# Decoder layer kernel: merge, output and down projections in token-major form, up projection on joined high and low halves

## The chip, the cores and the metric

The kernel runs on one core of a Trainium2 chip. The metric is the device time of one execution in microseconds (us); less is better.

## What is computed

One layer with 256 tokens, 2048 channels, all in fp32. In the reference, cut to what matters here:

```python
h = modulate(rms_norm(x, norm1_gain), shift1, scale1)
aq, ak, av, gq, gk, gv, gr, glr, ga, gb = split(h @ w_in)        # 2048 x 11792
merged = sigmoid(ga) * (y_attn @ w_branch_attn) + sigmoid(gb) * (y_gla @ w_branch_gla)
x = x + gate1 * (merged @ w_out)                                  # 2048 x 2048
h2 = modulate(rms_norm(x, norm2_gain), shift2, scale2)
u = h2 @ w_ffn_up                                                 # 2048 x 11264
y = conv_b + sum(conv_w[tap] * shifted(u, tap) for tap in 0..2)   # causal over tokens
a, b = split(y); x = x + gate2 * ((silu(a) * b) @ w_ffn_down)     # 5632 x 2048
```

shift, scale and gate (six vectors of 2048) come from `silu(c) @ w_ada + b_ada`, a vector times a 2048 x 12288 matrix.

## The kernel before

Every large product is done in units. A unit is 256 rows (two k-tiles of 128) by 512 columns of a weight matrix, 512 KB. SP loads it to one of four slots of `stage`; ScalarE rounds it to fp32r (`w_hi`, helper `hi`, L525); VectorE (DVE) subtracts (`w_lo`, helper `lo`, L766); TensorE multiplies. Activations are split in the same way into a high and a low half, and each product is three matmuls: hi x hi, lo x hi, hi x lo. SP may load unit k when the low half of unit k-4 is made (`lo_done`), ScalarE may round it when TensorE has used unit k-4 (`used`). The four engines run programs of their own, in an order written out by hand, which meet at semaphores.

In the *feature* form the weights stand in the array (128 columns at a time) and 256 tokens stream: 24 matmuls of 256 columns a unit (`unit`, L1161). In the *token* form, used for the GLA values, the activations of 128 tokens stand and 512 weight columns stream: 12 matmuls of 512 columns. The result of the first is channels by tokens, of the second tokens by channels. Results lie in two halves of PSUM (`ps`, parity `par`), each freed by `ps_free`.

The order: norm and modulation; queries and keys; GLA queries, keys, values; attention between them; the GLA gate; then **merge** (4 turns of 28 units: gate a, gate b, attention branch, GLA branch; L1406), **output** (2 turns of 16 units, L1423), the second norm, **up** (11 turns of 16 units, L1442) and **down** (2 turns of 44 units, L1453). Beside the units the modulation is accumulated: tiles `ada` of w_ada (512 KB each, 192 in all) are multiplied by c on DVE (`times_c`, L777) and added up over partitions by TensorE (`reduce_mod`, L1195), 16 tiles to a chunk of 1024 values; chunks 7 to 10 go beside the merge, chunk 11 beside the output projection. After each merge turn ScalarE and DVE split the merged tiles (`m_hi`, L700, `m_lo`, L1034). `x` is stored in feature order to HBM early (L393) and re-read into `x1` for the residual, which SP issues 12 units ahead of the output projection (L440). After the output projection the squares are summed (ScalarE L711, DVE L1063 and L1066), TensorE adds them over partitions, ScalarE makes the root, and tile by tile DVE, ScalarE and DVE again make `h2_hi` and `h2_lo` (L1082, L721, L793), each freeing one unit of the up projection's first block. In the up projection ScalarE and DVE take the convolution straight from PSUM (L737, L1104, L1108). In the down projection DVE adds gate and residual (L1136), TensorE transposes the result to token order (`back`, L1456), ScalarE copies it (L537), SP stores it.

## Time and profile before

| | |
|---|---|
| time, median of 3 runs | 1770.29 us (1768.89 to 1773.26) |
| span of the profiled execution | 1765.9 us (the page gives no other time of it) |
| TensorE, matmuls, busy | 1652.6 us, 94% |
| DVE busy | 1137.1 us, 64% |
| ScalarE busy | 775.7 us, 44% |
| HBM read | 384.26 MB, 221 GB/s over the span |
| mean granted clock of TensorE | 0.961 of full speed |

Matmuls are pipelined, and their ends are modelled: a record of 0.28 us may follow the last one after 0.12. So the price of one is the length of an unbroken stretch over its number. The granted clock is 1.00 or 0.50 of full speed (2.4 or 1.2 GHz). "Issue" is time in which an engine waited for nothing that the profile shows.

### The profile page before, as it was taken

Reading aid. Unit: us, or ns where it says so; the run is one execution under the profiler, and the core shown is the slowest. Engines: PE = TensorE matmul, PEld = TensorE weight load, DVE = VectorE, ACT = ScalarE, POOL = GpSimd, SP = SyncE. Lnnn points to the kernel's source line nnn. Section 1 sums busy time; section 2 is a strip of 40 time slices with the busy share of each in tenths; the row PEclk is TensorE's granted clock in tenths of the full one; section 3 lists DMA queues with packets and bytes.
Section 4 is the critical chain, followed back from the end, with each engine's and each line's share of the span. In section 5 each row is a group of like instructions: output and inputs, shape, how many; then the busy total and the mean of one; then the engine's idle time right before and its main releaser. Section 6 shows DMA issues by size and latency. Waiting matters only on the chain.

```text
span 1765.9 us, 33321 instructions
## 1 busy us (share of the span) xinstructions
PE 1652.6 (94%) x13089; PEld 1617.8 (92%) x13089; DVE 1137.1 (64%) x1192; ACT 775.7 (44%) x906; POOL 78.9 (4%) x52
## 2 busy tenths in 40 slices
PE   3185999999999999999999899999999999999999
PEld 3185999877999999999999899999999999998998
DVE  5797366598787686767687666666666555544443
ACT  3022433576675434333344545444445444433332
POOL 3052000000121000000000000000000000000000
PEclk8596899999999999999999899999999999999999
DMA  8978658576667878878888466666666666656553
GB/s 262 344 255 284 229 191 274 184 245 208 210 216 233 285 277 286 289 274 295 277 303 276 134 186 179 182 185 179 182 186 179 182 186 180 183 170 196 173 165 129
DMA packets 180117, 390.79 MB, mean 221 GB/s; under 512 B 13970, under 2 KB 18622, under 8 KB 179534
## 3 DMA queue, kind: packets, MB, share of 16 engines
q1 hardware_dynamic: 180046, 389.82, 68.7%
q8 instruction: 48, 0.79, 0.2%
q14 instruction: 23, 0.19, 0.0%
HBM read 384.26 MB, written 5.25 MB: 221 GB/s over the span
## 4 chain that ended last, share of the span: by engine, by line
PE 88%; DVE 6%; DMA 4%; ACT 1%; issue 1%; SPq 0%; DVEq 0%; ACTq 0%
PE ps L1144 83%; PE b L1144 5%; DMA ada<-in_w_ada 3%; DVE acc L777 3%; DVE acc_odd L777 1%; DVE h_lo L793 1%; DMA vrows<-in_ffn_conv_w 0%; DVE xn L818 0%; DMA stage<-in_w_in 0%; DVE w_lo L766 0%; PE b L1315 0%; PE ps L1223 0%; ACT w_hi L525 0%; PE b L1460 0%; ACT p L644 0%
## 5 line engine op out<-in xcount | busy, mean ns | idle before, releaser
L766 DVE TENSOR_TENSOR w_lo<-stage,w_hi 128x1024 fp32r<-128x1024 f32 x512 | 628.7, 1231 | 509.3 <-ACT w_hi L525 507.0
L525 ACT ACTIVATE w_hi<-stage 128x1024 fp32r<-128x1024 f32 x528 | 556.4, 1058 | 798.7 <-PE ps L1144 685.8
L1144 PE MATMUL ps<-h_hi,w_hi 128*128 128x256 f32 x2528 | 722.7, 286 | 16.6 <-DVE h_lo L793 16.6
L1144 PE MATMUL ps<-h_lo,w_hi 128*128 128x256 f32 x2528 | 718.9, 284 | 0.0
L1144 PE MATMUL ps<-h_hi,w_lo 128*128 128x256 f32 x2528 | 718.7, 284 | 0.0
L1144 PEld LDWEIGHTS ps<-h_hi,w_hi 128*128 128x128 f32 x2528 | 488.5, 193 | 18.8 <-issue 12.0
L1144 PEld LDWEIGHTS ps<-h_lo,w_hi 128*128 128x128 f32 x2528 | 488.6, 193 | 0.9 <-issue 0.8
L1144 PEld LDWEIGHTS ps<-h_hi,w_lo 128*128 128x128 f32 x2528 | 488.5, 193 | 0.0
L777 DVE SCALAR_TENSOR_TENSOR acc<-ada,cact,acc 128x1024 f32<-128x1024 f32 x156 | 220.8, 1415 | 6.5 <-DMA ada<-in_w_ada 3.8
L1144 PE MATMUL ps<-g_hi,w_hi 128*128 128x256 f32 x704 | 200.6, 285 | 4.1 <-issue 4.1
L1144 PE MATMUL ps<-g_lo,w_hi 128*128 128x256 f32 x704 | 200.2, 284 | 0.0
L1144 PE MATMUL ps<-g_hi,w_lo 128*128 128x256 f32 x704 | 200.2, 284 | 0.0
L1144 PEld LDWEIGHTS ps<-g_hi,w_hi 128*128 128x128 f32 x704 | 136.2, 193 | 4.3 <-issue 4.3
L1144 PEld LDWEIGHTS ps<-g_lo,w_hi 128*128 128x128 f32 x704 | 136.2, 193 | 0.0
L1144 PEld LDWEIGHTS ps<-g_hi,w_lo 128*128 128x128 f32 x704 | 136.1, 193 | 0.0
L1144 PE MATMUL ps<-m_hi,w_hi 128*128 128x256 f32 x256 | 72.6, 284 | 0.0
L1144 PE MATMUL ps<-m_lo,w_hi 128*128 128x256 f32 x256 | 72.5, 283 | 0.0
L1144 PE MATMUL ps<-m_hi,w_lo 128*128 128x256 f32 x256 | 72.5, 283 | 0.0
L1144 PE MATMUL ps<-yg_hi,w_lo 128*128 128x256 f32 x256 | 72.5, 283 | 0.0
L1144 PE MATMUL ps<-yg_lo,w_hi 128*128 128x256 f32 x256 | 72.5, 283 | 0.0
L1144 PE MATMUL ps<-yg_hi,w_hi 128*128 128x256 f32 x256 | 72.5, 283 | 0.0
L1144 PE MATMUL ps<-w_hi,h_hi 128*128 128x512 f32 (+1 forms) x160 | 62.1, 388 | 0.0
(231 smaller groups left out, 1699.6 us busy)
## 6 DMA issues: line engine op xcount, KB each, us to landing
ada<-in_w_ada SPq DMA_DIRECT2D x192, 512.0 KB, 5.1
stage<-in_w_in SPq DMA_DIRECT2D x184, 512.0 KB, 4.1
stage<-in_w_ffn_up SPq DMA_DIRECT2D x176, 512.0 KB, 3.7
stage<-in_w_ffn_down SPq DMA_DIRECT2D x88, 512.0 KB, 4.5
...
x_tok<-in_x SPq DMA_DIRECT2D x1, 2048.0 KB, 7.6
```

The costliest lines, as they stand in the source:

```text
L525: act.activation(w_hi[:, u.slot(k)], stage[:, u.slot(k)], ACT.Copy).then_inc(hi_done, 1)
L766: TT(w_lo[:, u.slot(k)], stage[:, u.slot(k)], w_hi[:, u.slot(k)].bitcast(F32), ALU.subtract).then_inc(lo_done, 1)
L777: STT(out=to[:], in0=ada[:, a.slot(k)], scalar=cc, in1=to[:], op0=ALU.mult, op1=ALU.add).then_inc(ada_done, 1)
L793: f = STT(out=x_lo[:, kt], in0=xn(kt), scalar=shift(kt), in1=x_hi[:, kt].bitcast(F32), op0=ALU.add, op1=ALU.subtract)
L1144: return pe.matmul(out, lhsT, rhs, start=start, stop=stop, skip_group_check=True)
```

## The change

- Merge, output and down projection go to the token form (`token_unit`). The gates are multiplied in token order, so gate1 and gate2 are needed as rows on all partitions: `spread_mod` reduces a chunk by two matmuls with a matrix of ones, `take_gate` adds the bias, which SP loads spread over the partitions. `MOD_TILE` puts the gates at the places of chunks 8 to 11 in time.
- The merged tiles are transposed back by TensorE (`merged_back`) one turn later, and split by `merged_hi` and `merged_lo`.
- x is no longer stored in feature order; x itself is re-read, after output unit 2 in SP's order and after the last merge unit is used.
- The second norm works on token-major `x1`: sums by ScalarE's accumulator (`square_sums`), scaling, transposes (`xn2` to `ps`), then `h2`, whose high and low halves lie side by side.
- Up projection (`up_unit`): one matmul of 512 columns with w_hi against both halves, one of 256 with w_lo against the high half, added into the right half of the bank; ScalarE copies that half to `up`, DVE adds the left half, and the convolution reads `up`. It uses all eight PSUM banks in two sets.
- Down: four blocks in straight code and four pairs of banks, results in token order at once, no transposes, stores by 128 tokens. Merge and output are straight code too.

```diff
-MOD_TILE = (0, 16, 8, 24, 32, 40, 48, 56, 64, 72, 80, 88)
+MOD_TILE = (0, 16, 8, 24, 48, 56, 64, 72, 32, 40, 80, 88)
+R_GATE1, R_GATE2 = 8, 10
+MERGE_EXTRA = ((1, 1, 1, 2), (1, 1, 1, 2), (), (1, 2, 1, 2))
+WOUT_EXTRA = ((1, 2, 1, 2), (1, 1, 1, 2), (1, 1, 1, 2), ())
...
-    x1 = sb("x1", 0, [P, KT, T])
-    h2_hi = sb("h2_hi", 16, [P, KT, T], F32R)
-    h2_lo = sb("h2_lo", 32, [P, KT, T], F32R)
+    x1 = sb("x1", 0, [P, 2, D])
+    h2 = sb("h2", 16, [P, KT, 2, T], F32R)
...
+    up = sb("up", 192, [P, NT, T])
+    ytmp = sb("ytmp", 16, [P, 2, 2, NB])
+    outs = sb("outs", 24, [P, 4, 2, NB])
...
+    psum = nc.alloc_psum_tensor("ps", [P, 8, NB], F32)
+    ps = psum[:, 0:4].rearrange("p (b c) (j t) -> p b (c j) t", b=2, t=T)
+    b4 = psum[:, 4]
+    b56 = psum[:, 5:7].rearrange("p c (j t) -> p (c j) t", t=T)
+    b7 = psum[:, 7]
+    ps_tok = psum[:, 0:4].rearrange("p (b a) n -> p b a n", b=2)
...
-            sp.wait_ge(xT_act, 2)
-            sp.wait_ge(xT_dve, 3)
-            sp.dma_start(xs, xT[:]).then_inc(xs_out, 16)
...
+                if i == 0:
+                    sp.wait_ge(yg_ready, 4)
+                    gate_bias(gate1[:], 2 * KT).then_inc(gate1_in, 16)
+            a = Run(KT * 11)
+            kt = 0
+            for b in range(4):
+                u = Run(U_WOUT + 8 * b)
+                for k in range(8):
+                    load(u, k, wo_u[k][:, :, b * NB:(b + 1) * NB])
+                    if b == 0 and k == 2:
+                        sp.wait_ge(used, U_WOUT)
+                        sp.dma_start(x1[:], x_t).then_inc(x_back, 16)
+                        gate_bias(gate2_b[:], 5 * KT).then_inc(gate2_in, 16)
+                    for _ in range(WOUT_EXTRA[b][k - 4] if k >= 4 and WOUT_EXTRA[b] else 0):
+                        load_ada(a, kt, kt, mod_cols(11), ada_out)
+                        kt += 1
...
-            def results_out(b):
-                act.wait_ge(y_tr, b + 1)
-                if b >= 2:
-                    act.wait_ge(stored, 16 * (b - 1))
-                act.activation(outs[:, b % 2], b56[:].rearrange("p (a j) t -> p a (j t)", a=2), ACT.Copy).then_inc(outs_ready, 1)
...
+            def merged_hi(i):
+                act.wait_ge(m_tr, i + 1)
+                act.activation(m_hi[:, 4 * i:4 * i + 4], b56, ACT.Copy).then_inc(mhi_done, 1)
...
+            def square_sums(b):
+                act.wait_ge(x1_done, b + 1)
+                for t in range(2):
+                    act.activation(sq_junk[:], x1[:, t, b * NB:(b + 1) * NB], ACT.Square, accum_out=ssq[:, t, b:b + 1]).then_inc(x1sq_done, 1)
+                    act.wait_ge(x1sq_done, 2 * b + t + 1)
+            for b in range(4):
+                u = Run(U_WOUT + 8 * b)
+                for k in range(AHEAD, 8 + AHEAD):
+                    hi(u, k)
+                    if b == 0 and k == AHEAD + 3:
+                        merged_hi(3)
+                    if b and k == AHEAD + 3:
...
+            square_sums(3)
             act.wait_ge(n2_sum, 1)
-            rstd_of(rs2[:], b7[:, 0:T], D).then_inc(n2_rstd, 1)
+            rstd_of(rs2[:], rs2[:], D).then_inc(n2_rstd, 1)
...
+                    act.activation(up[:], psum[:, 4 * (1 - b):4 * (2 - b), T:2 * T], ACT.Copy).then_inc(lo_half, 1)
                     for k in range(8):
-                        if k < 2:
-                            for j in (2 * k, 2 * k + 1):
+                        hi(u, 8 + AHEAD + k)
+                        if k == 0:
+                            act.wait_ge(ps_free[1 - b], i + (18 + b))
...
+            def take_gate(r, dst, bias_row, half):
+                dve.wait_ge(mod_red, r + 1)
+                lo_cols, hi_cols = (slice(half * ADA_W + n * NB, half * ADA_W + (n + 1) * NB) for n in range(2))
+                own(TT(dst[:, lo_cols], b4, bias_row[:, lo_cols], ALU.add))
+                TT(dst[:, hi_cols], b7, bias_row[:, hi_cols], ALU.add).then_inc(mod_ready, 1)
...
+            def merged_lo(i):
+                dve.wait_ge(mhi_done, i + 1)
+                TT(m_lo[:, 4 * i:4 * i + 4], b56, m_hi[:, 4 * i:4 * i + 4].bitcast(F32), ALU.subtract).then_inc(m_done, 1)
...
+                for k in range(AHEAD, 7 + AHEAD):
+                    lo(u, k)
+                    for _ in range(WOUT_EXTRA[b][k - 4] if k < 8 and WOUT_EXTRA[b] else 0):
+                        times_c(a, kt, kt, acc_out, kt == 0, ada_out)
+                        kt += 1
+                    if b == 0 and k == AHEAD + 3:
+                        merged_lo(3)
+                    if b == 3 and k == AHEAD + 5:
+                        take_gate(11, gate2, gate2_b, 1)
+                dve.wait_ge(x_back, 16)
+                dve.wait_ge(mod_ready, 10)
+                dve.wait_ge(used, u.at(8))
+                TT(gated[:], ps_tok[:, par], gate1[:, cols].unsqueeze(1).broadcast_to([P, 2, NB]), ALU.mult).then_inc(ps_free[par], 1)
+                dve.wait_ge(ps_free[par], 16 + (b + 1) // 2)
+                TT(x1[:, :, cols], gated[:], x1[:, :, cols], ALU.add).then_inc(x1_done, 1)
+                dve.wait_ge(x1_done, b + 1)
+                if b == 0:
+                    dve.wait_ge(gate2_in, 16)
+                    take_gate(10, gate2, gate2_b, 0)
+                if b == 1:
+                    dve.wait_ge(mod_ready, 8)
+                    own(STT(out=a2[:], in0=mod[:, 4 * KT:5 * KT], scalar=1.0, in1=V_G2, op0=ALU.add, op1=ALU.mult))
+                lo(u, 7 + AHEAD)
...
+            dve.wait_ge(x1sq_done, 8)
+            dve.tensor_reduce(rs2[:], ssq[:], AX.X, ALU.add).then_inc(n2_sum, 1)
             dve.wait_ge(n2_rstd, 1)
-            def h2_lo_of(pair):
-                lo_of(lambda kt: xr[:, kt % 4], lambda kt: mod[:, 3 * KT + kt:3 * KT + kt + 1], h2_hi, h2_lo, pair, h2hi_done, h2_ready)
-            for pair in range(8):
+            def x1_scaled(g):
+                for t in range(2):
+                    f = TS(xn2[:, t, g * NB:(g + 1) * NB], x1[:, t, g * NB:(g + 1) * NB], rs2[:, t:t + 1], None, ALU.mult)
+                    own.note(f) if t == 0 else f.then_inc(xn2_done, 1)
+            def h2_f(pair):
                 if pair >= 2:
                     dve.wait_ge(h2_ready, pair - 1)
-                for kt in (2 * pair, 2 * pair + 1):
-                    f = STT(out=xr[:, kt % 4], in0=x1[:, kt], scalar=a2[:, kt:kt + 1], in1=rs2[:], op0=ALU.mult, op1=ALU.mult)
-                f.then_inc(h2f, 1)
+                dve.wait_ge(xn2_tr, pair // 2 + 1)
+                for j in range(2):
+                    kt = 2 * pair + j
+                    f = TS(xr[:, kt % 4], ps[:, pair // 2 % 2, kt % 4], a2[:, kt:kt + 1], mod[:, 3 * KT + kt:3 * KT + kt + 1], ALU.mult, ALU.add)
+                    own.note(f) if j == 0 else f.then_inc(h2f, 1)
+            def h2_lo_of(pair):
+                dve.wait_ge(h2f, pair + 1)
+                dve.wait_ge(h2hi_done, pair + 1)
+                for j in range(2):
+                    kt = 2 * pair + j
+                    f = TT(h2[:, kt, 1], xr[:, kt % 4], h2[:, kt, 0].bitcast(F32), ALU.subtract)
+                    own.note(f) if j == 0 else f.then_inc(h2_ready, 1)
+            x1_scaled(0)
+            x1_scaled(1)
+            for pair in range(8):
...
+                h2_f(pair)
+                if pair in (0, 2):
+                    x1_scaled(2 + pair // 2)
...
+                    dve.wait_ge(lo_half, i * 2 + (b + 1))
+                    TT(up[:], psum[:, 4 * (1 - b):4 * (2 - b), 0:T], up[:], ALU.add).then_inc(ps_free[par], 1)
...
-                    STT(out=ytmp[:, par, j], in0=ps[:, par, j], scalar=mod[:, 5 * KT + kt:5 * KT + kt + 1], in1=x1[:, kt], op0=ALU.mult, op1=ALU.add).then_inc(y_tile, 1)
+                    own(TT(ytmp[:, b % 2, t], psum[:, 2 * ((b + 2) % 4) + t], gate2[:, cols], ALU.mult))
+                    TT(outs[:, b, t], ytmp[:, b % 2, t], x1[:, t, cols], ALU.add).then_inc(outs_ready, 1)
...
+            def up_unit(u, k, b):
                 pe.wait_ge(lo_done, u.at(k + 1))
                 s = u.slot(k)
-                for j in range(NT):
-                    cols = slice(j * P, (j + 1) * P)
-                    for q in range(2):
-                        kt = 2 * k + q
-                        mm(ps[:, par, j], w_hi[:, s, q, cols], xh[:, kt], False)
-                        mm(ps[:, par, j], w_hi[:, s, q, cols], xl[:, kt], False)
-                        f = mm(ps[:, par, j], w_lo[:, s, q, cols], xh[:, kt], False, q == 1)
-                    if j == 1:
+                for q in range(2):
+                    kt = 2 * k + q
+                    for j in range(NT):
+                        cols = slice(j * P, (j + 1) * P)
+                        bank = psum[:, 4 * (1 - b) + j]
+                        mm(bank, w_hi[:, s, q, cols], h2[:, kt].rearrange("p a t -> p (a t)"), kt == 0)
+                        f = mm(bank[:, T:2 * T], w_lo[:, s, q, cols], h2[:, kt, 0], False, kt == KT - 1)
+                f.then_inc(used, 1)
+            def token_unit(u, k, out2, xh, xl, last, half_done=None):
+                pe.wait_ge(lo_done, u.at(k + 1))
+                s = u.slot(k)
+                order = [(q, t) for q in range(2) for t in range(2)]
+                if half_done is not None:
+                    order = [(q, t) for t in range(2) for q in range(2)]
+                for q, t in order:
+                    kt = 2 * k + q
+                    tok = slice(t * P, (t + 1) * P)
+                    mm(out2[:, t], xh[:, kt, tok], w_hi[:, s, q], kt == 0)
+                    mm(out2[:, t], xl[:, kt, tok], w_hi[:, s, q], False)
+                    f = mm(out2[:, t], xh[:, kt, tok], w_lo[:, s, q], False, last and q == 1)
+                    if half_done is not None and (q, t) == (1, 0):
                         f.then_inc(half_done, 1)
                 f.then_inc(used, 1)
...
+            def spread_mod(r, sums):
+                pe.wait_ge(ada_done, (r + 1) * KT)
+                pe.wait_ge(mod_ready, r)
+                mm(b4, ones[:], sums[:, 0:NB], True, True)
+                mm(b7, ones[:], sums[:, NB:2 * NB], True, True).then_inc(mod_red, 1)
...
+            def merged_back(i):
+                pe.wait_ge(mrg_ready, i + 1)
+                for j in range(NT):
+                    for t in range(2):
+                        f = pe.transpose(b56[:, j, t * P:(t + 1) * P], mrg[:, t, j * P:(j + 1) * P], ident[:])
+                f.then_inc(m_tr, 1)
...
+            for b in range(4):
+                par = (1 + b) % 2
+                u = Run(U_WOUT + 8 * b)
+                free(par, 15 + (b + 1) // 2)
+                for k in range(8):
+                    if b == 0:
+                        pe.wait_ge(m_done, 4 if k >= 6 else k // 2 + 1)
+                    token_unit(u, k, ps_tok[:, par], m_hi, m_lo, k == 7)
+                    if b == 0 and k == 1:
+                        merged_back(3)
+                    if b == 3 and k == 4:
+                        spread_mod(11, acc_out)
+            for g in range(4):
+                pe.wait_ge(xn2_done, g + 1)
+                if g >= 2:
+                    pe.wait_ge(h2f, 2 * (g - 1))
+                for j in range(NT):
+                    for t in range(2):
+                        cols = slice((NT * g + j) * P, (NT * g + j + 1) * P)
+                        f = pe.transpose(ps[:, g % 2, j, t * P:(t + 1) * P], xn2[:, t, cols], ident[:])
+                f.then_inc(xn2_tr, 1)
+            pe.wait_ge(mod_ready, 12)
             with pe.Fori(0, UP_STEPS) as i:
                 for b in range(2):
                     par = (1 + b) % 2
...
-                def back(b):
-                    for j in range(NT):
-                        pe.wait_ge(y_tile, i * 8 + (4 * b + j + 1))
-                        for t in range(2):
-                            f = pe.transpose(b56[:, 2 * t + j // 2, (j % 2) * P:(j % 2 + 1) * P],
-                                             ytmp[:, (1 + b) % 2, j, t * P:(t + 1) * P], ident[:])
-                    f.then_inc(y_tr, 1)
-                for b in range(2):
-                    par = (1 + b) % 2
-                    u = Run(U_DOWN + DOWN_UNITS * b, i, 2 * DOWN_UNITS)
-                    pe.wait_ge(ps_free[par], 28 + b)
-                    for k in range(DOWN_UNITS):
-                        if b == 0 and k % 2 == 0:
-                            pe.wait_ge(g_ready, k // 2 + 1)
-                        if k < DOWN_UNITS - 1:
-                            unit(u, k, par, g_hi, g_lo, False)
-                        else:
-                            last_unit(u, k, par, g_hi, g_lo, down_half)
-                        if b == 1 and k == 1:
-                            back(0)
-                back(1)
...
+            for b in range(4):
+                u = Run(U_DOWN + DOWN_UNITS * b)
+                if b % 2 == 0:
+                    pe.wait_ge(ps_free[1 - b // 2], 28 + b // 2)
+                for k in range(DOWN_UNITS):
+                    if b == 0 and k % 2 == 0:
+                        pe.wait_ge(g_ready, k // 2 + 1)
+                    out2 = psum[:, 2 * ((b + 2) % 4):2 * ((b + 2) % 4) + 2]
+                    token_unit(u, k, out2, g_hi, g_lo, k == DOWN_UNITS - 1, down_half if k == DOWN_UNITS - 1 else None)
```

`token_unit` is the old token branch of `unit` with the three matmuls of each k-tile and token half; in its last unit of down it goes through the token halves one after the other and signals `down_half` after the first.

## Rows read from the trace of the kernel before

**Rows 1.** The page: busy time and share by engine; three groups (busy, mean ns).
```profile
PE 1652.6 (94%) x13089; PEld 1617.8 (92%) x13089; DVE 1137.1 (64%) x1192; ACT 775.7 (44%) x906; POOL 78.9 (4%) x52
...
L766 DVE TENSOR_TENSOR w_lo<-stage,w_hi 128x1024 fp32r<-128x1024 f32 x512 | 628.7, 1231 | 509.3 <-ACT w_hi L525 507.0
L525 ACT ACTIVATE w_hi<-stage 128x1024 fp32r<-128x1024 f32 x528 | 556.4, 1058 | 798.7 <-PE ps L1144 685.8
```

**Rows 2.** Waits: who waited for what, total us, times, longest.
```profile
ACT w_hi L525 <- PE ps L1144: 685.8, 420, 9.6
```

**Rows 3.** The chain in order of time: start us, us, what, number of instructions.
```profile
177.12 0.88 PE b L1144 x2
...
368.93 13.84 PE ps L1144 x60
...
556.31 80.74 PE ps L1144 x672
637.05 1.68 PE b L1144 x16
...
987.85 578.55 PE ps L1144 x4800
1566.41 0.87 PE b L1460 x8
...
1702.68 57.60 PE ps L1144 x480
```

**Rows 4.** Windows: start:end length, busy us of each engine, clock, DMA share, GB/s.
```profile
45.00:83.00 38.00, 7.12 (x32) 6.98 (x32) 27.18 (x24) 0.00 (x0) 0.00 (x0) 0.50 0.95 338
720.00:803.00 83.00, 83.00 (x696) 83.00 (x695) 58.71 (x50) 33.00 (x32) 0.00 (x0) 1.00 0.80 280
```

**Rows 5.** DMA issues: count, KB each, median us from issue to landing.
```profile
x_tok<-in_x SPq DMA_DIRECT2D x1, 2048.0 KB, 7.6
```

**Rows 6.** Groups of DVE and ScalarE from 186 us on, shapes apart (busy, mean ns).
```profile
L777 DVE SCALAR_TENSOR_TENSOR acc<-ada,cact,acc 128x1024 f32<-128x1024 f32 x126 | 163.6, 1298 | 0.6
...
L1104 DVE SCALAR_TENSOR_TENSOR cvb<-ps,vec,cvb 128x255 f32<-128x255 f32 x44 | 19.1, 477 | 0.0
...
L1063 DVE TENSOR_TENSOR sqsum<-sqsum,xsq 128x512 f32<-128x512 f32 x4 | 2.8, 693 | 0.0
...
L775 DVE TENSOR_SCALAR acc<-ada,cact 128x1024 f32<-128x1024 f32 x2 | 1.5, 747 | 0.0
...
L711 ACT ACTIVATE xsq<-x 128x512 f32 x8 | 5.0, 631 | 9.4 <-DVE x L1059 9.4
...
L644 ACT ACTIVATION_READ_ACCUMULATOR p<-p,nmx 128x1 f32 x16 | 3.0, 187 | 0.0
```

**Rows 7.** Timeline from output to up projection: start us, us, instructions, idle before.
```profile
978.09 1.84 PE L1144 MATMUL b<-ones,acc 128*128 128x1 f32 x16
...
983.06 1.28 ACT L530 ACT_TABLE_LOAD   x1
...
987.85 0.58 PE L1144 MATMUL ps<-h_hi,w_hi 128*128 128x256 f32 x1 [5.86 <-DVE h_lo L793]
```

**Rows 8.** Timeline between the two turns of the down projection.
```profile
1624.86 1.61 PE L1460 MATMUL b<-ident,ytmp 128*128 128x128 f32 x8
...
1630.57 0.58 PE L1144 MATMUL ps<-g_hi,w_hi 128*128 128x256 f32 x1 [4.10 <-issue]
```

**Rows 9.** Windows with the granted clock, after two pauses.
```profile
990.00:993.00 3.00, 3.00 (x16) 3.00 (x16) 2.93 (x8) 1.82 (x4) 0.00 (x0) 0.50 0.00 0
993.00:996.00 3.00, 3.00 (x26) 3.00 (x26) 2.96 (x8) 1.51 (x4) 0.00 (x0) 0.98 0.00 0
1633.00:1636.00 3.00, 3.00 (x20) 3.00 (x19) 0.00 (x0) 0.33 (x1) 0.00 (x0) 0.70 0.00 0
```

**Rows 10.** Timeline: the issue of the last store.
```profile
1762.76 0.38 SPq L343 DMA_DIRECT2D out<-outs  x1
```

**Rows 11.** Timeline of SP's queue: the store of x in feature order.
```profile
146.22 9.71 SPq L393 DMA_DIRECT2D x_featuremajor<-xT  x1
```

296 lines of the change are left out of this document (119 added, 177 removed).

## The prediction

> **What bounds the kernel now.** Read first the busy times of the page and then the waits. TensorE is busy for 94% of the span, DVE for 64% [rows 1], and the longest wait of the whole kernel is ScalarE waiting for TensorE to finish with a weight slot before it rounds the next unit [rows 2]. So a unit (256 rows by 512 columns of weights, 512 KB) is ready before TensorE wants it, and time goes where TensorE's stream goes. The third view is the chain in order of time [rows 3]: long stretches of nothing but matmuls. From it come the prices. A matmul of 256 columns follows the last one after 80.74/672 = 0.1202 us in the merge and 57.60/480 = 0.1200 us in the down projection. One of 512 columns (the token form, which the kernel already uses for the GLA values) takes 13.84/60 = 0.2307 us. Two of the short ones are 0.2403 us: the long form saves 9.6 ns for the same products. This small difference, taken some thousand times, is the whole gain of the change; what it pays is at the seams between stages, so those are read closest.
>
> **Wide streaming in merge, output and down.** A unit was 24 matmuls of 256 columns, 2.884 us (2.880 in down); it becomes 12 of 512, 2.768 us. Merge 112 units x 0.116 = 12.9; output 32 x 0.116 = 3.7; down 88 x 0.112 = 9.9. Sum -26.5 us, all on TensorE's own path. Weights and activations change places only; the rounding and the DMAs per unit stay as they are.
>
> The Trainium skill, page "TensorE: Matmul & The Clock Gate", section "Back-to-back issue gap", gives 262 cycles for 256 columns and 518 for 512, so that a long matmul would save about 2.5 ns and not 9.6. By it the wide form would bring an estimated 7 us in these three stages, and 3.5 us in the up projection. The chain's rows at both widths disagree and decide.
>
> **Up projection.** Per k-tile and column tile, three matmuls of 256 become one of 512 (w_hi on both halves) and one of 256 (w_lo): 8 x (0.2307 + 0.1200) = 2.806 us against 2.880. 176 units x 0.074 = -13.1 us. The two widths alternating is not in the trace. If each matmul costs its columns and the extra of a short one (13.5 ns over 256 columns at 2.4 GHz, 106.7 ns), a unit is 2.776 us and the gain 18; with the extra of a long one on both (17.4 ns), 2.838 us and 7.4. I take the middle. New here is the eviction: ScalarE copies the right halves out (about 1.06 us, as its rounding of the same size), DVE adds the left ones (1.23, as the subtraction of the same size [rows 1]), and only then do the convolution steps start. Behind these wait ScalarE's rounding of unit 12, which can't start before a further unit has run anyway (2.8 us), and DVE's subtraction behind it. Unit 12's w_lo is then ready about 5 us after the half step's end, and TensorE wants it after four units, 11.2 us. DVE has per half step 8 x 1.23 + 8 x 0.48 [rows 6] + 1.23 for the sum + 1.2 for half of the gated product and its low half = 16.1 us of work in 22.4. I cost it at nothing; without that cover it is 1.06 + 1.23 us on each of 22 half steps.
>
> **Small work on TensorE.** The merged tiles must now be transposed back, 4 x 8 transposes at 0.87 us per eight [rows 3]: +3.5. Two such groups in the middle of the down projection go: -1.7. A modulation chunk's reduction to a spread row is two fp32 matmuls of 512 columns, 2 x 0.88, for 1.68 before [rows 3]: +0.3 over four. The last chunk's reduction moves from the pause after the output projection into its stream: +1.8. Sum +3.9.
>
> **The seam merge to output.** SP used to re-read x well ahead. Now it blocks after output unit 2 until the last merge unit is used (call it T), and then issues x (2 MB), the gate-2 bias spread over the partitions (1 MB) and, behind them, the weights of unit 3. x in 2 MB took 7.6 us to land [rows 5]. For the rest I take the best rate the trace shows, 338 GB/s at 95% share [rows 4]: 3.1 us for 1 MB, 1.55 us for each 512 KB. Unit 3 lands at T+12.3, is rounded (1.06) and subtracted (1.23) [rows 1], ready at T+14.7. TensorE does the chunk's reduction (1.8), units 0 and 1, the transposes (0.9) and unit 2, and wants unit 3 at T+11.0. Worse is unit 6: it waits for the last merged tiles' low halves, which DVE makes after unit 7's subtraction and two modulation steps. With the six modulation tiles of this block queued between the weights, unit 7 lands at T+24.7, its w_lo is there at 27.2, two steps of 1.30 [rows 6] and the subtraction of 1.23 end at T+31.0. TensorE would want unit 6 at T+19.3: +11.7 us in all. After a pause the clock is at half (0.50, 1.2 GHz) for a while: the up projection started so at 987.85 and had 0.50 to some 993 us [rows 9], 5.2 us at half speed, 2.6 lost. I add 2.3. The seam: +14.0. Below, were the DMAs no limit, unit 6 would still be 0.6 us late by the steps alone (1.06 + 1.23 + 2 x 1.30 + 1.23 = 6.1 us from the end of unit 3, against two units of 2.77); above, 17.5 with the slower average rate of the merge, 280 GB/s [rows 4]. I take the fast rate because nothing but the queued transfers asks for the DMA then. In the merge the same rate leaves room: 44 tiles of 0.52 MB in 80.1 us are 288 GB/s, and the extra 1 MB for the gate-1 bias is 3 us against a lead of three units. No cost.
>
> The Trainium skill, page "DMA: Bandwidth & Descriptors", section "Anatomy of one DMA", fits a transfer as 2.0 us plus its bytes at 436 GB/s. By it, unit 3 would land at an estimated T+10.4 and nearly hide; no stretch here reaches that rate, 338 is the most.
>
> **The seam output to up.** Before, TensorE's last output matmul was done at 978.1 and the up projection began at 987.85: 9.8 us, with one more table load in it [rows 7]. Now: product with the gate 1.23, add 1.23, two squares with their sums 2 x (0.63 + 0.19) [rows 6], reduction, Ln, table load 1.28 [rows 7] and Exp on two columns, some 6.5 us with the hand-overs. Then DVE works in this order before the last transposes may go: four scalings of x1 (each two of 128x512; a tensor-scalar of 1024 took 0.75, so 0.8 per pair), four pairs of h2 from PSUM (0.9), two low halves (0.9): 8.6 us. The last eight transposes at half clock take 1.7, and the program puts all of them ahead of the first up matmul. 17.2 us, +7.4. Bounds +4 (scalings and transposes overlap better, full clock) and +10 (scalings at 0.69 per tile).
>
> **The down projection's loop.** Between its two turns TensorE stood from the end of unit 21 (1624.86) to 1630.57: eight transposes stretched to 1.61, then 4.10 of "issue" [rows 8], then half clock until about 1634.8 [rows 9], 2.1 lost. Now the four blocks are straight code in four pairs of banks, and nothing there waits. -7.8. If the issue stall belongs to instruction supply and comes back in the straight stream, only 1.6 of it go.
>
> **The end.** The last matmul was done at 1760.28, the store issued at 1762.76 [rows 3, 10], the span ends at 1765.9. Now token half 0 is evicted while half 1 runs, then two DVE steps of 0.69 [rows 6] and the store: -1.1.
>
> **Removed early.** The store of x in feature order kept SP for 9.71 us at 146 us [rows 11]. The weights behind it came late, but TensorE was then held by DVE's h_lo, and later by the key norm's ScalarE steps, so only up to 1 us could come back. I take 0.
>
> **Sum.** -26.5 - 13.1 + 3.9 + 14.0 + 7.4 - 7.8 - 1.1 = -23.2 us against the profiled span of 1765.9, which gives 1742.7. The page has no time for this execution but its span; the median of the runs, 1770.29, lies 4.4 us over it, for what is around the span, and I keep that: 1747.1.
>
> **Rivals.** *The refill hides* (0.17): the DMAs after T come fast enough or the reader of unit 6 doesn't wait for so much; then the seam costs about 1 and the time is 1734. For it speaks that the kernel's lead is three units; against, that 3 MB go ahead of a weight whose lead is already spent. *Smaller gains* (0.19): the alternating widths cost 17.4 ns each (+5.7) or the issue stall stays (+6.2): 1753 to 1759. For it: neither is shown by the trace. *Columns are all that counts* (0.04): if a 512-column matmul with a new stationary tile each time cost twice the short one, 0.2403 us, the 39.6 us of streaming gains vanish and the seams remain: 1747.1 + 39.6 = 1786.7, slower. It decides from 0.2364 us per long matmul on, where gains and seams cancel. Against it stands the measured 0.2307, three times alike in the GLA stage. The skill's section on the issue gap leans this way, with most of the gain gone. *My forecast* (0.60): 1747.1, between 1740 and 1754.
>
> The range of 1732 to 1761 takes in the first two rivals. A measurement of this kernel tells about 0.3% (5.3 us) from no change. Faster 0.91, same 0.05, slower 0.04.
>
> **What would show it.** In the profile after: merge stretches of 336 matmuls in 77.5 us; up at 2.81 us a unit; a pause of TensorE before output unit 3 (some 4 us) and a larger one before unit 6, ended by m_lo, with the x load landing some 8 us after SP's wait; 17 us between output and up; no pause in down. What would make it wrong: long matmuls over 0.236 us, DVE or ScalarE ending waits of TensorE in the up loop, or a refill that does not stall.

## The result and the profile after

The changed kernel takes 1728.66 us (median of 4 executions, 1728.59 to 1737.05) against 1771.25 of the kernel before; ratio 0.977, 95% interval 0.974 to 0.979. The forecast was 1747.1 with a range down to 1732. The sign and the mechanisms were right, the gain was 42.6 us where 23.2 was forecast: too small by nearly a half.

The span of the profiled execution is 1726.9 us, 39.0 less than the 1765.9 of before, and its time is 1728.59: 1.7 us lie around the span. Of the miss 2.7 us are the anchor: the forecast set the median of three runs over the span of one execution and took the 4.4 us between them for what lies around it. Executions of the kernel before with their own spans beside them have 1.7 to 2.8, so the profiled one was quicker than the median.

The page after, busy time and the two costly groups of the up projection (busy, mean ns):

```profile
PE 1607.0 (93%) x8877; PEld 1395.9 (81%) x8877; DVE 1165.2 (67%) x1205; ACT 792.7 (46%) x932; POOL 78.6 (5%) x52
...
L1179 PE MATMUL ps<-h,w_hi 128*128 128x512 f32 x1408 | 490.2, 395 | 0.0
L1179 PE MATMUL ps<-h,w_lo 128*128 128x256 f32 x1408 | 390.9, 278 | 0.0
```

TensorE has 8877 matmuls instead of 13089 [rows 1] and is busy for the same share. The chain of the kernel after, in order of time (start us, us, what, number of instructions), shows where it stands still:

```profile
640.66 0.87 PE ps L1468 x8
641.53 77.95 PE ps L1179 x340
...
799.20 70.75 PE ps L1179 x312
869.97 0.37 SPq L445
...
870.89 11.11 DMA stage<-in_w_out
...
883.11 1.24 DVE w_lo L773
884.36 9.08 DMA stage<-in_w_out
...
895.70 1.29 DVE acc_out L784
897.09 1.28 DVE acc_out L784
898.37 1.15 DVE m_lo L1022
899.56 75.44 PE ps L1179 x316
975.08 1.06 ACT w_hi L533
...
991.28 1.94 PE ps L1509 x8
993.22 728.08 PE ps L1179 x3866
1721.40 0.70 DVE ytmp L1170
```

A merge turn is now 0.87 for the transposes of the turn before plus 77.95 us; it was 80.74 plus 1.68 [rows 3]. From 869.97 (SP stops waiting for the last merge unit and issues x) the chain leaves TensorE: DMA, DVE, DMA, two modulation steps, m_lo. From 993.22 on it is TensorE alone, with no pause at all, where before the down projection stood still between its turns [rows 8]. Stage by stage, from the first matmul of one to the first of the next (before, after, difference, forecast of the difference):

| stretch | before | after | difference | forecast |
|---|---|---|---|---|
| start to merge | 556.3 | 556.9 | +0.6 | 0 |
| merge with its reductions | 329.7 | 314.8 | -14.9 | -10.0 |
| output | 92.1 | 103.4 | +11.3 | +13.0 |
| pause before up | 9.8 | 18.1 | +8.3 | +7.4 |
| up and down | 772.4 | 729.5 | -42.9 | -32.5 |
| end | 5.7 | 4.2 | -1.5 | -1.1 |

The forecast of a stretch is the sum of the terms that fall into it. The seams came out as forecast, within 2 us. What was too small are the two rows in which nothing but matmuls counts.

### The profile page after: what moved, and what is told of

Same layout as the page of the kernel before. It is cut to its first block, busy times and chain, and to the rows that moved or that the text cites. A ratio compares the mean times of both kernels' runs of the same rounds, so it can differ in the third digit from the quotient of the medians.

```text
span 1726.9 us, 23736 instructions
## 1 busy us (share of the span) xinstructions
PE 1607.0 (93%) x8877; PEld 1395.9 (81%) x8877; DVE 1165.2 (67%) x1205; ACT 792.7 (46%) x932; POOL 78.6 (5%) x52
## 4 chain that ended last, share of the span: by engine, by line
PE 86%; DVE 6%; DMA 5%; ACT 1%; issue 1%; SPq 0%; DVEq 0%; ACTq 0%
PE ps L1179 85%; DMA ada<-in_w_ada 3%; DVE acc L784 3%; DMA stage<-in_w_out 1%; DVE acc_odd L784 1%; DVE h_lo L807 1%; PE ps L1280 0%; DVE xn L832 0%; DMA vrows<-in_ffn_conv_w 0%; DMA stage<-in_w_in 0%; ACT w_hi L533 0%; PE ps L1509 0%; DVE w_lo L773 0%; PE ps L1372 0%; DVE xr L1102 0%
## 5 line engine op out<-in xcount | busy, mean ns | idle before, releaser
L1179 PE MATMUL ps<-h,w_hi 128*128 128x512 f32 x1408 | 490.2, 395 | 0.0
L1179 PE MATMUL ps<-h,w_lo 128*128 128x256 f32 x1408 | 390.9, 278 | 0.0
L1179 PEld LDWEIGHTS ps<-h,w_hi 128*128 128x128 f32 x1408 | 265.0, 188 | 61.6
L1179 PEld LDWEIGHTS ps<-h,w_lo 128*128 128x128 f32 x1408 | 265.4, 188 | 0.0
L1179 PE MATMUL ps<-h_hi,w_hi 128*128 128x256 f32 x672 | 197.3, 294 | 16.3 <-DVE h_lo L807 10.9
L1179 PE MATMUL ps<-h_lo,w_hi 128*128 128x256 f32 x672 | 193.1, 287 | 0.0
L1179 PE MATMUL ps<-h_hi,w_lo 128*128 128x256 f32 x672 | 193.1, 287 | 0.0
L1179 PEld LDWEIGHTS ps<-h_hi,w_hi 128*128 128x128 f32 x672 | 132.3, 197 | 19.1 <-DVE h_lo L807 6.7
L1179 PEld LDWEIGHTS ps<-h_lo,w_hi 128*128 128x128 f32 x672 | 132.2, 197 | 1.1 <-issue 1.0
L1179 PEld LDWEIGHTS ps<-h_hi,w_lo 128*128 128x128 f32 x672 | 132.1, 197 | 0.0
```

Of the source, the lines that this page charges most:

```text
L1179: return pe.matmul(out, lhsT, rhs, start=start, stop=stop, skip_group_check=True)
```

## The price of a matmul

The starts of single matmuls settle it. Timeline of TensorE in the kernel before, GLA values, where the forecast took its price from (start us, length of the record us):

```profile
370.12 0.40 PE L1144 MATMUL ps<-w_lo,h_hi 128*128 128x512 f32 x1
370.35 0.39 PE L1144 MATMUL ps<-w_hi,h_hi 128*128 128x512 f32 x1
370.58 0.39 PE L1144 MATMUL ps<-w_hi,h_lo 128*128 128x512 f32 x1
370.81 0.39 PE L1144 MATMUL ps<-w_lo,h_hi 128*128 128x512 f32 x1
371.03 0.39 PE L1144 MATMUL ps<-w_hi,h_hi 128*128 128x512 f32 x1
```

Three of them, one group of three products, take 0.68 us (370.35 to 371.03), 0.2267 each, not 0.2307. The forecast divided a piece of the chain, 13.84 us, by its 60 matmuls [rows 3]. Such a piece ends with the modelled end of its last matmul, 0.4 us after its start, and not where the next would start, 0.23 after it. Over 60 matmuls that is 3 ns each, and the first few of the piece took 0.231 to 0.236, which is the fourth. Against a difference of 9.6 ns between two short ones and a long one these 4 ns are much. Over 672 short ones the same end makes 0.1202 of 0.1200. With 0.2267 and 0.1200 a unit costs 2.720 us instead of 2.880: 112 x 0.160 = 17.9 in the merge, 32 x 0.160 = 5.1 in the output projection and 88 x 0.160 = 14.1 in down, 37.1 us in all instead of 26.5, and the up projection's pair costs 0.3467 instead of 0.3507. To see whether the width and not the form or the seams makes the difference, two runs took the width away.

**Down projection in 256 columns, same form.**

```diff
-                    mm(out2[:, t], xh[:, kt, tok], w_hi[:, s, q], kt == 0)
-                    mm(out2[:, t], xl[:, kt, tok], w_hi[:, s, q], False)
-                    f = mm(out2[:, t], xh[:, kt, tok], w_lo[:, s, q], False, last and q == 1)
+                    step = 256 if u.base >= U_DOWN else NB
+                    for x, w, first in ((xh, w_hi, kt == 0), (xl, w_hi, False), (xh, w_lo, False)):
+                        for n in range(0, NB, step):
+                            f = mm(out2[:, t, n:n + step], x[:, kt, tok], w[:, s, q, n:n + step], first and n == 0, last and q == 1 and w is w_lo)
```

> The changed kernel, but in the down projection each matmul of 512 columns is issued as two of 256, with the same stationary tile and in the same token form. Theory A (each matmul costs its columns at 2.4 GHz plus one fixed extra of some 13.4 ns, whatever its width): 24 x 0.1200 = 2.880 us a unit again, against 12 x 0.2267 = 2.720 now, so 88 x 0.160 = 14 us longer than the changed kernel, span about 1741. Theory B (the long form costs 0.2307 us as the forecast had it, and the unforeseen gain lies at the seams): 88 x 0.112 = 10 us longer, 1737. Theory C (not the width but the token form itself is cheaper): nothing or a few us, under 1732.

Measured: from the first up matmul to the last half block the chain has 741.42 us against 728.08, +13.3. Windows of the down projection, this kernel and then the changed one (length, busy us with instructions of TensorE, weight loads, DVE, ScalarE, GpSimd, clock, DMA share, GB/s):

```profile
1500.00:1600.00 100.00, 100.00 (x835) 100.00 (x835) 46.54 (x40) 37.23 (x37) 0.00 (x0) 1.00 0.59 189
```

```profile
1500.00:1600.00 100.00, 100.00 (x443) 82.84 (x442) 48.98 (x42) 38.87 (x37) 0.00 (x0) 1.00 0.62 199
```

835 matmuls in 100 us are 0.120 us each, 443 are 0.226. A window counts every matmul whose record reaches into it, one or two more than start in it, so such a quotient is up to 0.5% low; from start to start, over the same stage, they are 0.1200 and 0.2267. The missing 0.7 us are the half clock at the start of up, which ended at 997.9 here, 2.7 us after that start, and at 997.3 in the changed kernel, 4.1 us after. Theory A, with 14, stands; B (10) and C (nothing) fall. The token form as such gives nothing, the width everything.

**Up projection in three matmuls of 256, new eviction kept.**

```diff
-                        mm(bank, w_hi[:, s, q, cols], h2[:, kt].rearrange("p a t -> p (a t)"), kt == 0)
+                        mm(bank[:, 0:T], w_hi[:, s, q, cols], h2[:, kt, 0], kt == 0)
+                        mm(bank[:, T:2 * T], w_hi[:, s, q, cols], h2[:, kt, 1], False)
```

> The changed kernel, but the up projection issues the product of w_hi with the joined halves as two matmuls of 256, so three of 256 per tile as before; the eviction with the extra copy and add stays. Theory A: 8 x 3 x 0.1200 = 2.880 us a unit against 2.773 now, 176 x 0.107 = 19 us longer, span about 1746. Theory B (forecast's price): 13 us longer, 1740. If the new eviction costs TensorE anything, the up stretch is longer than the 2.880 us a unit of the kernel before; I expect no wait of TensorE on DVE or ScalarE in it.

Measured: 746.21 us for the same piece, +18.1 (A: 19, B: 13). 836 matmuls in 100 us here (first row) and as many in the kernel before (second row), so the added copy and sum cost TensorE nothing, as forecast:

```profile
1200.00:1300.00 100.00, 100.00 (x836) 100.00 (x835) 64.97 (x76) 52.09 (x61) 0.00 (x0) 1.00 0.64 182
```

```profile
1200.00:1300.00 100.00, 100.00 (x836) 100.00 (x835) 62.15 (x80) 49.05 (x57) 0.00 (x0) 1.00 0.63 181
```

**Other widths.** Four matmuls of 128 in the first down block (the edit above with another `step`); in another kernel 384 + 128 in the first block and 320 + 192 in the second.

```diff
+                    step = 128 if u.base >= U_DOWN and u.base < U_DOWN + DOWN_UNITS else NB
```

```diff
+                    cuts = ((0, 384, 512), (0, 320, 512))[(u.base - U_DOWN) // DOWN_UNITS] if U_DOWN <= u.base < U_DOWN + 2 * DOWN_UNITS else (0, 512)
+                    for x, w, first in ((xh, w_hi, kt == 0), (xl, w_hi, False), (xh, w_lo, False)):
+                        for n, m in zip(cuts, cuts[1:]):
+                            f = mm(out2[:, t, n:m], x[:, kt, tok], w[:, s, q, n:m], first and n == 0, last and q == 1 and w is w_lo)
```

> The changed kernel, but the first of the four down blocks (22 units) issues each matmul of 512 as four of 128. Theory A (columns plus 13.4 ns) gives 48 x 66.7 ns = 3.20 us a unit, 22 x 0.48 = 10.6 us longer. Rival: a new stationary tile can't come faster than the transposes of 128 columns showed, 0.87/8 = 0.109 us; then 48 x 0.109 = 5.2 us a unit, 22 x 2.5 = 55 us longer.

> The changed kernel, but in the first down block each matmul of 512 is cut to 384 and 128, in the second to 320 and 192. With a price of columns at 2.4 GHz plus 13.4 ns, but never under 0.120 us: 0.173 + 0.120 = 0.293 us a pair, 3.52 us a unit in the first block, and 0.160 + 0.120 = 0.280, 3.36 us a unit in the second. Without the floor both would be 0.240 us, 2.88 a unit. If the fixed part shrinks behind a short one, as 0.115 for 256 behind 512 in the up projection hints, the pairs are some 5 ns cheaper.

```profile
1510.00:1590.00 80.00, 80.00 (x719) 80.00 (x718) 21.50 (x19) 16.82 (x16) 0.00 (x0) 1.00 0.32 99
```

```profile
1490.00:1550.00 60.00, 60.00 (x421) 60.00 (x420) 25.63 (x24) 18.95 (x18) 0.00 (x0) 1.00 0.50 153
1560.00:1620.00 60.00, 60.00 (x470) 60.00 (x469) 23.35 (x20) 21.13 (x20) 0.00 (x0) 1.00 0.60 178
```

128 columns: 80/719 = 0.111 us each, from start to start 0.1117, the rival's price and not the 0.067 of theory A alone. The pair 384 + 128 takes 0.2865 us (first row: 60/(421/2) = 0.285; the block of 264 pairs runs from 1481.51 to 1557.14), the pair 320 + 192 takes 0.2568 (second row: 60/(470/2) = 0.255; 264 pairs from 1557.14 to 1624.93). One rule fits all within 2 ns: columns at 2.4 GHz plus 13.3 ns, and never under 0.1117 us. It gives 0.1733 + 0.1117 = 0.285 and 0.1467 + 0.1117 = 0.258. Only 128, 256 and 512 columns have a stretch of their own; for 192, 320 and 384 the split of the pair is the rule's, and what the 13.3 ns and the floor are no run shows. (The expectation has two slips: it took 0.120 for the floor, and 0.160 for 320 columns, which are 0.133 + 0.013. Its 0.115 for 256 behind 512 doesn't hold either: from start to start the quicker pairs in the up projection take 0.3466, which is 0.2267 + 0.1200. And the kernel with 128 columns is 67.4 us longer over up and down, of which some 9 lie in its up loop, told of below.) So 256 columns, at 0.1200, are above the floor, and the 13.3 ns are paid once per matmul, as often as the columns are cut. That they are the same at 256 and 512 is what the forecast's bound of 2.776 us a unit for the up projection had assumed; measured are 490.2 us from the first up matmul (992.87) to the first of down, less 2.2 for the half clock at its start, over 176 units: 2.773.

## The seam merge to output

Timeline of SP and ScalarE of the kernel after, around the last merge unit:

```profile
869.97 0.37 SPq L445 DMA_DIRECT2D x<-in_x  x1
870.38 0.47 SPq L340 DMA_DIRECT2D gate_b<-in_b_ada  x1
870.89 1.05 SPq L322 DMA_DIRECT2D stage<-in_w_out  x2
```

```profile
882.02 1.06 ACT L533 ACTIVATE w_hi<-stage 128x1024 fp32r<-128x1024 f32 x1 [13.64 <-DMA stage<-in_w_out]
...
893.47 1.06 ACT L533 ACTIVATE w_hi<-stage 128x1024 fp32r<-128x1024 f32 x1 [1.58 <-DMA stage<-in_w_out]
```

With T = 869.9 the weights of unit 3 are there at T+12.1 (forecast 12.3), their low half at 14.4 (14.7); unit 7 lands at T+23.5 (24.7) and m_lo ends at T+29.6 (31.0). TensorE waited twice, before unit 3 and before unit 6:

```profile
884.48 0.57 PE L1179 MATMUL ps<-w_hi,m_hi 128*128 128x512 f32 x1 [3.69 <-DVE w_lo L773]
...
899.56 0.79 PE L1179 MATMUL ps<-w_hi,m_hi 128*128 128x512 f32 x1 [5.04 <-DVE m_lo L1022]
```

3.69 and 5.04 us, and its clock fell with each, so that output unit 3 and unit 6 began at half speed (0.69 of full speed in the third row below, 0.50 in the last). The second wait takes in what the first and its half clock had cost, since m_lo comes when it comes: TensorE was 10.6 us late at unit 6 (forecast 11.7), and the half clock behind it, to some 905.2, lost 2.8 (forecast 2.3).

By the Trainium skill, page "DMA: Bandwidth & Descriptors", section "Anatomy of one DMA" (2.0 us plus the bytes at 436 GB/s, a fit that the page gives for transfers issued by GpSimd; here SP issues them), unit 3 would have landed at an estimated T+10.4; the run shows 12.1.

The forecast's "best rate the trace shows", 338 GB/s, was a misreading: it is the mean over 38 us [rows 4], and windows of 5 us in the kernel before show more (first two rows). The changed kernel reached 405 with 3 MB queued at once (next rows).

```profile
75.00:80.00 5.00, 0.68 (x4) 0.68 (x4) 3.20 (x3) 0.00 (x0) 0.00 (x0) 0.50 1.04 411
80.00:85.00 5.00, 2.90 (x14) 2.81 (x14) 3.15 (x7) 0.58 (x2) 0.00 (x0) 0.50 1.04 406
```

```profile
875.00:880.00 5.00, 5.00 (x28) 4.21 (x27) 0.00 (x0) 0.00 (x0) 0.00 (x0) 1.00 0.99 405
880.00:885.00 5.00, 1.31 (x6) 0.77 (x5) 1.77 (x2) 2.11 (x2) 0.00 (x0) 0.97 1.00 372
885.00:890.00 5.00, 5.00 (x17) 3.97 (x16) 4.15 (x5) 1.06 (x1) 0.00 (x0) 0.69 1.04 404
...
900.00:903.00 3.00, 3.00 (x8) 2.32 (x8) 1.77 (x2) 0.00 (x0) 0.00 (x0) 0.50 0.40 74
```

The landing times came out all the same, since most of the sum was x itself. DMA issues of the changed kernel (KB, us to landing):

```profile
x<-in_x SPq DMA_DIRECT2D x1, 2048.0 KB, 7.7
```

7.7 us (forecast 7.6), and the 1.5 MB behind it landed 4.3 us later, at 882.0, which is 366 GB/s (forecast 4.65 at 338).

Three runs bear on the causes. The measure is the stretch from the third unit of the last merge turn (right behind the transposes) to the end of the output projection: 175.9 us in the changed kernel (799.20 to 975.08), 173.6 to 175.9 in the profiles of six others that have the same code there.

**x re-read earlier.**

```diff
+            sp.wait_ge(used, U_WOUT - 12)
+            sp.dma_start(x1[:], x_t).then_inc(x_back, 16)
+            sp.wait_ge(used, U_WOUT - 8)
+            gate_bias(gate2_b[:], 5 * KT).then_inc(gate2_in, 16)
...
-                    if b == 0 and k == 2:
-
+                    if b == 0 and k == 4:
                         sp.wait_ge(used, U_WOUT)
-                        sp.dma_start(x1[:], x_t).then_inc(x_back, 16)
-                        gate_bias(gate2_b[:], 5 * KT).then_inc(gate2_in, 16)
```

> The changed kernel, but SP issues the re-read of x as soon as its place is free (12 units before the output projection, where the kernel before had it) and the gate-2 bias 4 units later; only the first modulation tile of the output projection still waits for the last merge unit. If the seam costs what the forecast worked out (unit 3 behind 3 MB, then unit 6 behind the queue), both waits of TensorE go but for some 0.7 us, and so does the half clock behind them: 12 to 13 us less than the changed kernel, the stretch from the last merge unit to the last output matmul 92 to 93 us instead of 105. If the seam is bound by DVE's order (two modulation steps ahead of m_lo) and not by the transfers, only the 4 us before unit 3 go.

Measured: 169.6 us, 4 to 6 less and not 12. The timeline of TensorE still has both waits, 1.63 and 3.50 us:

```profile
877.56 0.47 PE L1180 MATMUL ps<-w_hi,m_hi 128*128 128x512 f32 x1 [1.63 <-DVE w_lo L774]
...
898.56 0.50 PE L1180 MATMUL ps<-w_hi,m_hi 128*128 128x512 f32 x1 [3.50 <-DVE m_lo L1023]
```

x was issued at 861.9, only 12 us ahead of T (874.2), since SP has to issue all merge loads first; it then stood in front of output weights in a DMA that was busy (0.99 share, 392 GB/s between 865 and 875 us). Issuing the same 3 MB 12 us earlier moves the wait and takes a part of it. My expectation was wrong in this: the condition of the wait is met 12 units ahead, but SP's order lets x go only 12 us ahead. (In the kernel before it was the same, 14 us: issued at 871.68, output projection at 885.99; there 2 MB went and not 3.) And the second wait still ends with m_lo, behind unit 7 and two modulation steps.

**The last merged tiles split two units earlier**, ahead of unit 5's modulation steps.

```diff
-                    if b == 0 and k == AHEAD + 3:
+                    if b == 0 and k == AHEAD + 1:
                         merged_hi(3)
```

(and `merged_lo` likewise, ahead of the modulation steps)

> The changed kernel, but ScalarE and DVE split the last merged tiles two units earlier in their order, ahead of the modulation steps of unit 5. Unit 3 is late as before (T+14.4). Unit 6 then waits for its own weights alone, which landed at T+19.9 or so and are ready 2.4 us later; TensorE reaches it after unit 5, at T+23. So the second wait, 6 us, goes nearly whole, with some of the half clock: 6 to 8 us less in that stretch.

Measured: 168.3 us, 5.3 to 7.6 less; the second wait is 0.41 us and now ends with the weights:

```profile
888.30 0.64 PE L1179 MATMUL ps<-w_hi,m_hi 128*128 128x512 f32 x1 [3.39 <-DVE w_lo L773]
...
904.17 0.47 PE L1179 MATMUL ps<-w_hi,m_hi 128*128 128x512 f32 x1 [0.41 <-DVE w_lo L773]
```

**x in four pieces, one per output block, the bias in two, modulation tiles moved from the first block to the later ones, and the early split.**

```diff
-WOUT_EXTRA = ((1, 2, 1, 2), (1, 1, 1, 2), (1, 1, 1, 2), ())
+WOUT_EXTRA = ((0, 0, 1, 2), (2, 2, 1, 2), (1, 2, 1, 2), ())
...
+                    if k == 1:
+                        if b == 0:
+                            sp.wait_ge(used, U_WOUT - 12)
+                        sp.dma_start(x1[:, :, b * NB:(b + 1) * NB], x_t[:, :, b * NB:(b + 1) * NB]).then_inc(x_back[b], 16)
+                    if k == 3 and b in (0, 2):
+                        half = b // 2
+                        if b == 0:
+                            sp.wait_ge(used, U_WOUT - 8)
...
+                    if b == 0 and k == 6:
                         sp.wait_ge(used, U_WOUT)
```

> The changed kernel, but the re-read of x comes in four pieces of 512 KB, one for each output block and only just ahead of its use, the gate-2 bias in two of 512 KB; the modulation tiles are moved from the first output block to the later ones (3, 7, 6 instead of 6, 5, 5), and the last merged tiles are split two units earlier. No transfer stands in front of a weight for long, none is needed at once: if volume ahead of the weights is what stalled TensorE at the seam, both waits and the half clock behind them go, 13 us less in the stretch from the last merge unit to the last output matmul (105 to 92). If something else binds there (ScalarE's or DVE's order), 6 to 8 us go, as when only the split came earlier.

```profile
797.24 77.95 PE ps L1189 x340
875.18 0.87 PE ps L1478 x8
876.06 83.42 PE ps L1189 x364
959.57 1.06 ACT w_hi L542
...
977.71 727.97 PE ps L1189 x3866
```

From 797.24 to 959.57 are 162.3 us, 13.5 less than the changed kernel and at least 11.3 less than in each profile that has the changed kernel's code there. The chain doesn't leave TensorE in this stretch at all. So the seam's cost of 14.0 in the forecast was right in size. Moving the volume ahead alone took 4 to 6 us of it, moving m_lo ahead in ScalarE's and DVE's order alone 5 to 8, this kernel the whole; neither of the first two alone is enough. What the pieces, the bias in halves and the moved modulation tiles each give in it was not taken apart.

## The pause before the up projection

The second norm's transposes in all eight banks, so that none waits for DVE to empty one:

```diff
-                if g >= 2:
-                    pe.wait_ge(h2f, 2 * (g - 1))
...
-                        f = pe.transpose(ps[:, g % 2, j, t * P:(t + 1) * P], xn2[:, t, cols], ident[:])
+                        f = pe.transpose(ps8[:, (g + 2) % 4, j, t * P:(t + 1) * P], xn2[:, t, cols], ident[:])
...
             pe.wait_ge(mod_ready, 12)
+            pe.wait_ge(h2f, 4)
```

> The changed kernel, but the second norm's transposes use all eight banks, so none of them waits for DVE to empty a bank; the first up matmul waits only until the first four pairs are taken from PSUM. The pause from the last output matmul to the first up matmul (18 us) loses the last group of transposes, 1.9 us at half clock. If TensorE's order and not DVE's were the limit it would lose more than 4.

Measured: from 972.74 to 989.35, 16.6 us against 18.1, 1.5 less. What is left in the chain there are steps of ScalarE and DVE one behind the other, and transposes; no run shortened these. Both seams mended at once:

> The same as the run with x in pieces, and the second norm's transposes in all eight banks. Both edits act on different seams and should add: 13 + 1.5 = 14.5 us less than the changed kernel, about 1714, with the up loop at either of its two paces (8 to 10 us apart). If the gain of the one is eaten at the other, the pause before the up projection is longer than 16.6 us.

The stretch over the output projection is 162.3, the pause 16.6 us: the gains add. The median of 6 executions is 1720.85, ratio 0.970 (0.967 to 0.973), better than the changed kernel; but the executions run from 1709.7 to 1728.5, and its profile fell on 1728.53.

## The straight code

One edit to the kernel before: the loop over the two turns of the down projection written out on TensorE.

```diff
-            with pe.Fori(0, 2) as i:
+            for i in range(2):
```

> The kernel before, with one edit: TensorE's loop of two turns over the down projection is written out. If the 4.1 us of issue between the two turns belong to the loop's edge, the pause falls to the eight transposes and the wait for DVE (1.6 us) and the half clock after it is gone: 4.1 + 2.1 = 6.2 us less, span about 1760. If it belongs to the supply of instructions at that place, it stays or moves, span 1766.

```profile
992.81 578.44 PE ps L1144 x4800
...
1629.70 1.61 PE b L1460 x8
1631.31 69.12 PE ps L1144 x576
```

TensorE goes on at 1631.31, right behind the transposes, where before it stood 4.10 us in "issue" [rows 8], and the clock stays at full speed. First up matmul to last output: 766.1 us against 772.4 before, -6.3 for 6.2 expected. The median of 8 executions is 1765.32, ratio 0.996 (0.994 to 0.997). The stall belonged to the loop's edge. Why the loops of the merge and the up projection have none at theirs stays open.

## What was not expected: two paces of one loop

The up loop of the changed kernel, a 512 and a 256 by turns, ran at one of two paces. Windows of two kernels with the same up loop, the changed one and the one with the transposes in eight banks:

```profile
1010.00:1450.00 440.00, 440.00 (x2540) 384.80 (x2539) 301.05 (x357) 242.77 (x280) 0.00 (x0) 1.00 0.65 189
```

```profile
1010.00:1450.00 440.00, 440.00 (x2493) 381.66 (x2492) 294.79 (x349) 240.01 (x277) 0.00 (x0) 1.00 0.64 186
```

2540 matmuls in 440 us (a pair takes 0.3466 us from start to start) or 2493 (0.3533), evenly over the whole loop, with no pause and at full clock in both. The quicker pace is just the sum of the two prices, 0.2267 + 0.1200; the slower one has 6.7 ns more in each pair, 176 x 8 of them, 9.4 us in the up loop: 2.827 us a unit, near the forecast's upper bound of 2.838. Of nine profiles with this order five had the quicker pace and four the slower, without regard to the edits, which touch other stages. The times would fit it, though only profiled executions show their pace: 1728.6 to 1728.7 three times and 1737.05 once for the changed kernel, 1709.7 to 1715.8 three times and 1725.9 to 1728.5 three times for the kernel with both seams mended. The profiled execution of the changed kernel had the quicker one. Each kernel's spread has a second source, the first 150 us, which wait for loads: the end of the first merge turn lies between 638.7 and 647.8 us in kernels that are the same up to there. That is why the readings above go by stretches. The whole times of all kernels:

| kernel | executions | us | pace in the profile |
|---|---|---|---|
| changed | 4 | 1728.6 to 1737.1 | quicker |
| down in 256 columns | 4 | 1740.1 to 1757.0 | quicker |
| up in three of 256 | 4 | 1747.7 to 1751.9 | (no pairs) |
| 128 columns in one down block | 1 | 1799.5 | slower |
| 384 + 128 and 320 + 192 | 1 | 1750.9 | quicker |
| before, straight down | 8 | 1759.3 to 1768.5 | (no pairs) |
| x early | 4 | 1719.9 to 1728.2 | quicker |
| m_lo early | 1 | 1733.1 | slower |
| transposes in eight banks | 1 | 1734.3 | slower |
| x in pieces | 1 | 1713.0 | quicker |
| both seams mended | 6 | 1709.7 to 1728.5 | slower |
| changed, grouped | 5 | 1729.2 to 1736.9 | (grouped) |
| both seams mended, grouped | 5 | 1716.7 to 1722.3 | (grouped) |

The single executions with m_lo early and with eight banks are longer than the changed kernel's median, although their own stretches are shorter: both have the slower pace, and the first also a merge that begins 4 us later.

A run grouped a unit's matmuls, first the eight of 512, then the eight of 256.

```diff
-                for q in range(2):
...
+                for wide in (True, False):
+                    for q in range(2):
...
+                            if wide:
+                                mm(bank, w_hi[:, s, q, cols], h2[:, kt].rearrange("p a t -> p (a t)"), kt == 0)
+                            else:
+                                f = mm(bank[:, T:2 * T], w_lo[:, s, q, cols], h2[:, kt, 0], False, kt == KT - 1)
```

> The changed kernel, but a unit of the up projection issues its eight matmuls of 512 first and its eight of 256 after them, instead of by turns. In the profiles so far the up loop ran at one of two paces, by execution and not by kernel: about 5.79 matmuls a us (pairs of 0.3455 us: the 256 in 0.115) or 5.67 (0.3527 us: the 256 in 0.120), 8 to 10 us apart over the loop. If the pair's cost is a fixed price per matmul, the grouped order gives 8 x 0.2268 + 8 x 0.1200 = 2.774 us a unit, as the faster pace does, in every execution, and the spread of the runs shrinks. If the short one gains only behind a long one, seven of eight lose that: 8 x 0.2268 + 0.115 + 7 x 0.120 = 2.769 at best, with the 512s in a row at the merge's price. If the two paces are a matter of when the loop starts, they stay.

> The run with x in pieces and the eight-bank transposes, with the grouped order of the up projection. The paces by turns gave 728 us (first up matmul to the last half block) in some executions and 738 in others; the grouped order gave 731.5 in its one profile, 575.5 matmuls in 100 us. If grouping fixes the pace, the up loop has 573 to 577 matmuls in 100 us again and the executions lie in one cluster near 1710 to 1716 (what is left of spread comes from the first 150 us, which are bound by loads), against two clusters 10 us apart without it. If the two paces stay, there are two clusters here too.

```profile
1010.00:1450.00 440.00, 440.00 (x2523) 387.27 (x2523) 295.91 (x348) 240.41 (x275) 0.00 (x0) 1.00 0.65 188
```

```profile
1010.00:1450.00 440.00, 440.00 (x2522) 387.21 (x2521) 300.82 (x357) 241.63 (x278) 0.00 (x0) 1.00 0.65 188
```

The same pace in both profiles: 2.792 us a unit, between the two paces and 19 ns over the sum of fixed prices. On the changed kernel, five executions took 1729.2 to 1736.9 (ratio 0.979, 0.977 to 0.981), which would fit either. On the kernel with both seams mended five took 1716.7 to 1722.3: a spread of 5.6 us against 18.8, and no second cluster. The median is 1721.11, ratio 0.971 (0.969 to 0.973). The expected 1710 to 1716 was too low: the grouped loop takes 3.4 us more than the quicker pace (731.46 us against 728.08 from the first up matmul to the last half block). So as far as two profiles and ten executions show, grouping gives up the quicker pace and avoids the slower; that it always does is not shown. The medians of the two versions can't be told apart. What sets the pace of an execution was not found.

## The prediction, step by step

- **What bounds it**: right. TensorE's own stream decided in every long stretch.
- **Wide streaming, -26.5**: this step failed. The mechanism was right, the price of the long matmul was not: the saving was taken as 9.6 ns; it is 13.3, since 0.2307 should have been 0.2267 (and 0.1202 in the merge 0.1200). It was -37.1, 10.6 more. The merge stretch agrees: -14.9 measured is 2.9 of small work less 17.8. By down in 256 columns the width gives 13.3 us there, against 9.9 in the forecast.
- **Up projection, -13.1**: the same mis-sized price; 176 x (2.880 - 2.773) = -18.8, 5.7 more. The bound from the short one's extra (2.776) was the true rule; I chose the middle of two bounds where one came from the faulty price. That the profiled execution had the quicker of two paces is luck; with the slower one the term would have been -9.4.
- **Small work, +3.9**: consistent with the stretches, not measured apart.
- **Seam merge to output, +14.0**: 11.3 for the whole output stretch, of which matmuls give -5.1 and small work +2.7 (0.9 and 1.8), so 13.7. Both waits, their order and what ended them were as forecast; the rate of 338 GB/s under it was not the best in the trace, but it priced only 4.65 us of the landing time.
- **Seam output to up, +7.4**: +8.3.
- **Down loop, -7.8**: the pause is gone; 6.3 of it shown by itself.
- **End, -1.1**: -1.5. **Removed early, 0**: +0.6, inside the spread of that part.
- **Anchor**: 2.7 us too high.

10.6 + 5.7 + 2.7 are 19.0 for 18.4 us missed; the other terms, most of them the pause before the up projection, give the rest back. The one execution with 1737.05 lies inside the range. Of the rivals, none happened in the profiled execution: the refill did stall, the gains were larger and not smaller, and the one in which only columns count was wrong in the other direction. But the alternating widths do cost nearly what *Smaller gains* feared (2.827 against 2.838 us a unit) in the executions with the slower pace, four of nine profiles.

The figures of the Trainium skill, page "TensorE: Matmul & The Clock Gate", section "Back-to-back issue gap", don't fit these fp32r matmuls, each with a stationary tile of its own (8877 weight loads for as many matmuls). The cycles that the forecast quoted, some 2.5 ns beside the columns, are the page's for an isolated matmul; for a stream of weight loads and matmuls it states 81 ns at 128 columns and 131 ns at 512. The runs show 111.7 and 226.7 ns, and 13.3 ns beside the columns at 256 and 512.

The range failed because it was widened for the seams, while the 39.6 us of streaming gains, some thousands of times a small difference of two prices, had hardly a range of their own.
